# A state-space step-size tile moved from the 13th to the 9th projection tile, with its logarithm work cut in three parts

## The reference

```python
u = rmsnorm(h, norm1_w[l])
proj = u @ w_in[l]                      # 1024 -> 6672 columns
hg_q, hg_f, hg_i, hg_g, m2_z, m2_xbc, m2_dt = jnp.split(proj, PROJ_SPLITS, axis=-1)
out_a = hgrn2_mixer(hg_q, hg_f, hg_i, hg_g, ...)
out_b = mamba2_mixer(m2_z, m2_xbc, m2_dt, ...)
# inside mamba2_mixer:
xbc = jax.nn.silu(causal_dwconv(xbc, conv_w, conv_b))     # 1536 channels, 4 taps
dt = jax.nn.softplus(dt_pre + dt_bias)                    # 16 heads
da = dt * (-jnp.exp(a_log))
a_cum = jnp.cumsum(chunks of da); decay_to_end = jnp.exp(a_cum[-1] - a_cum)
```

## Time and profile before

| | |
|---|---|
| median of 3 runs | 1690.28 us (1687.13 to 1690.29) |
| the profiled execution | 1689.66 us, its span in the trace 1687.9 us |
| TensorE busy | 1314.2 us (78%), 8402 matmuls |
| VectorE busy | 514.3 us (30%) |
| ScalarE busy | 480.1 us (28%) |
| GpSimd busy | 233.5 us (14%) |
| transfers | 524.01 MB, mean 310 GB/s |

### The profile page before, as it was taken

The page is one execution under the profiler, slowest core; times in us unless marked ns, Lnnn a source line. Parts: engine busy times, 40 slices in busy tenths (PEclk is TensorE's granted clock), DMA queues, the critical chain, the costliest instruction groups (busy, mean ns, idle before and its releaser), DMA issues.

```text
span 1687.9 us, 20870 instructions
## 1 busy us (share of the span) xinstructions
PE 1314.2 (78%) x8402; PEld 777.3 (46%) x8402; DVE 514.3 (30%) x944; ACT 480.1 (28%) x725; POOL 233.5 (14%) x101
## 2 busy tenths in 40 slices
PE   8989999999999999988656667666666655666665
PEld 5877788889998988843111111111111111111111
DVE  4864667436668445622000000000000000000001
ACT  5753566436564434722100001000000100000001
POOL 0000000029777654400000000000000000000000
PEclk9999999999999999997898777888977888797888
DMA  8846332268535542286999999999999999999997
GB/s 278 330 150 242 111 101 98 70 214 274 167 138 196 213 165 100 101 337 267 428 428 428 429 429 429 428 429 428 428 429 429 428 428 429 429 429 428 429 428 299
DMA packets 93919, 524.01 MB, mean 310 GB/s; under 512 B 8057, under 2 KB 32145, under 8 KB 66081
## 3 DMA queue, kind: packets, MB, share of 16 engines
q1 hardware_dynamic: 93521, 522.61, 76.4%
q10 hardware_dynamic: 336, 0.54, 0.1%
HBM read 522.08 MB, written 1.05 MB: 310 GB/s over the span
## 4 chain that ended last, share of the span: by engine, by line
DMA 47%; PE 42%; DVE 6%; ACT 3%; issue 1%; POOL 0%; SPq 0%; DVEq 0%; ACTq 0%
DMA ring<-in_w_down 23%; DMA ring<-in_w_up 23%; PE ps L691 6%; PE ps L695 6%; PE ps L692 6%; PE ps L915 5%; PE ps L1264 3%; PE ps L939 3%; PE ps L1286 3%; PE ps L1172 2%; PE ps L675 1%; PE ps L749 1%; DVE arena L2153 1%; PE ps L845 1%; ACT ring_r L1359 1%
## 5 line engine op out<-in xcount | busy, mean ns | idle before, releaser
L1264 PE MATMUL ps<-ring,arena 128*32 128x512 f32 x1984 | 294.1, 731 | 169.7 <-DMA ring<-in_w_up 120.0
L1716 POOL TENSOR_TENSOR ring_r<-ring,ring_r 128x1024 fp32r<-128x1024 f32 (+1 forms) x96 | 232.0, 2435 | 475.2 <-ACT ring_r L1359 475.2
L691 PE MATMUL ps<-arena_r,ring_r 128*128 128x258 f32 (+3 forms) x960 | 288.9, 301 | 8.7 <-PE ps L695 3.3
L695 PE MATMUL ps<-arena_r,ring_r 128*128 128x258 f32 (+3 forms) x960 | 280.9, 293 | 0.0
L1286 PE MATMUL ps<-ring,arena 128*32 128x512 f32 x960 | 161.6, 808 | 97.6 <-DMA ring<-in_w_down 91.4
L1264 PEld LDWEIGHTS ps<-ring,arena 128*32 128x32 f32 x1984 | 62.1, 122 | 369.6 <-DMA ring<-in_w_up 184.1
L691 PEld LDWEIGHTS ps<-arena_r,ring_r 128*128 128x128 f32 x960 | 182.8, 190 | 19.5 <-issue 13.3
L695 PEld LDWEIGHTS ps<-arena_r,ring_r 128*128 128x128 f32 x960 | 182.0, 190 | 2.8
L692 PE MATMUL ps<-arena_r,ring_r 128*128 128x256 f32 (+2 forms) x608 | 180.4, 297 | 0.0
L1359 ACT ACTIVATE ring_r<-ring 128x1024 fp32r<-128x1024 f32 (+1 forms) x122 | 126.0, 1037 | 40.0 <-PE ps L692 21.4
L1718 POOL TENSOR_TENSOR arena<-arena 128x512 f32<-128x512 f32 x1 | 1.3, 1320 | 975.0 <-ACT arena L1702 975.0
(11 more groups left out here) (395 smaller groups left out, 1452.7 us busy)
## 6 DMA issues: line engine op xcount, KB each, us to landing
ring<-in_w_gate SPq DMA_DIRECT2D x64, 2048.0 KB, 26.0
ring<-in_w_down SPq DMA_DIRECT2D x63, 2048.0 KB, 26.2
ring<-in_w_up SPq DMA_DIRECT2D x60, 2048.0 KB, 24.7
ring<-in_w_in SPq DMA_DIRECT2D x20, 2048.0 KB, 11.6
ring<-in_w_ada SPq DMA_DIRECT2D x12, 2048.0 KB, 8.8
ring<-in_ffn_w_up SPq DMA_DIRECT2D x22, 1024.0 KB, 7.9
ring<-in_w_out SPq DMA_DIRECT2D x6, 2048.0 KB, 8.2
ring<-in_ffn_w_down SPq DMA_DIRECT2D x4, 2048.0 KB, 8.4
```

Source lines behind the costliest of these rows:

```text
L691: pe.matmul(o, hi[:, k, :], r_(xhi(k0 + k)), start=first and k == 0, stop=False)
L695: mm = pe.matmul(o, lo[:, k, :], r_(xhi(k0 + k)), start=False, stop=last and k == nk - 1)
L1264: mm = pe.matmul(ps[32 * j:32 * j + 32, half, :], xs[:, kt, :], wk[:, 512 * j:512 * j + 512], start=kt == 0, stop=kt == KT - 1)
L1716: pool.tensor_tensor(r_(w), w, f_(rounded(c)), ALU.subtract).then_inc(ev("w_lo"), 1)
```

## The change

The dt tile is computed ahead of p8 and not ahead of p12. ScalarE's `dt_first` comes at j = 8. VectorE's `dt_rows` becomes four functions: `dt_logs` at j = 8, `dt_steps` at j = 9, `dt_sums` at j = 11, and `dt_rows_done` (the wait for the last Exp) at j = 14. On ScalarE the last two `conv_silu`, `dt_end` and the eviction of p12 stand together at j = 13, so that Silu, Exp and Sigmoid come in blocks. The operations themselves stay the same.

```diff
-            seq += ["dt"] * (j == 12) + [f"p{j}"]
+            seq += ["dt"] * (j == 8) + [f"p{j}"]
...
-                if j == 12:
+                if j == 8:
                     pe.wait_ge(ev("small_loaded"), 16 * 8)
                     o = open_tile("dt")
...
+            def evict_projection(j):
+
+                n, m = divmod(j, 4)
+                unit_ = ORDER[n]
+                fn = {0: ACT.Silu, 1: ACT.Sigmoid, 2: ACT.Copy, 3: ACT.Silu, 4: ACT.Silu}.get(unit_ // 2, ACT.Copy)
+                evict(f"p{j}", proj[:, 4 * unit_ + m, :], T, fn)
...
-                if 2 <= j <= 13:
+                if 2 <= j <= 11:
                     conv_silu(j - 2)
+                if j == 8:
+                    dt_first()
+                if j == 13:
+                    conv_silu(10)
+                    conv_silu(11)
+                    dt_end()
+                    evict_projection(12)
                 if j == 12:
-                    dt_first()
-                if j == 14:
-                    dt_end()
+                    continue
...
-                if j == 12:
-                    dt_rows()
+                if j == 8:
+                    dt_logs()
+                if j == 9:
+                    dt_steps()
+                if j == 11:
+                    dt_sums()
+                if j == 14:
+                    dt_rows_done()
```

More of the change, by code:

```diff
@@ L1510, in gate_squares @@
                     act.activation(proj[:, TX + 4 * g + k, :], proj[:, TZ + 4 * g + k, :], ACT.Square).then_inc(ev("squares"), 1)
+            def evict_projection(j):
[3 more added lines that the diff above has]
+                evict(f"p{j}", proj[:, 4 * unit_ + m, :], T, fn)
+                act.wait_ge(ev("tiles_freed"), TN[f"p{j}"] + 1)
+                if j < 12:
+                    act.activation(m2_t[:, j % 2, :], proj[:, TX + j, :], ACT.Identity, scale=pc("m2cw", 36 + j), bias=pc("m2cb", j)).then_inc(ev("proj_tiles"), 1)
+                else:
+                    act.nop().then_inc(ev("proj_tiles"), 1)
             for j in range(NPROJ):
@@ L1529, in _ @@
                     gate_squares(0)
[L1530 to L1537, removed]
+                evict_projection(j)
             root("mz0", T)
@@ L1830, in log1p_ends, with dt_logs @@
                 st.link(tt(lg, lg, tmp, ALU.add))
-            def dt_rows():
+            def dt_logs():
                 dve.wait_ge(ev("dt_in"), 1)
@@ L1841, in dt_rows, with dt_steps @@
                 dve.nop().then_inc(ev("log_arg"), 1)
+            def dt_steps():
                 dve.wait_ge(ev("log_log"), 1)
@@ L1845, in dt_rows, with dt_sums @@
                 st.link(ts(ch(4), ch(1), chan[:, 0, 2:3], -1.0, ALU.mult, ALU.mult))
+            def dt_sums():
                 st.link(dve.tensor_tensor_scan(ch(0), cs("reset", 16)[:, 3 * T:4 * T], ch(4), 0.0, ALU.mult, ALU.add))
@@ L1857, in dt_rows, with dt_rows_done @@
                 dve.nop().then_inc(ev("m2_end"), 1)
+            def dt_rows_done():
                 dve.wait_ge(ev("row_exp"), 4)
```

## The result

The changed kernel takes 1696.53 us (median of 7 runs, 1693.89 to 1698.31), the kernel before on the same chip 1689.71 us (7 runs, 1687.13 to 1691.72). The ratio is 1.0037, 95% interval 1.0027 to 1.0046: slower by 6.8 us where 3.8 us were forecast. A second measurement, on another chip (5 runs, and 24 of the kernel before), gave 1.0042 (1.0028 to 1.0055). The profiled execution, the slowest of the seven, took 1698.31 us around a span of 1696.5 us; before the span was 1687.9 us.

The account below looks back on a forecast made before the run. Bound by TensorE from 100 to 700 us, then by the experts' weight stream from 800 us. 6.6 us lost, 3.2 and 1.1 regained (+2.35), plus 1.4 for the clock: +3.8, so 1694.1 us; range 1690.3 to 1697.3.

Parts of the forecast that it names:

- ScalarE at j = 13, p15 at 87.9 instead of 81.3: p12's eviction stands behind Silu and Exp, so p15, which needs its bank, starts late and TensorE loses 6.6 us.
- VectorE's hand-over, `conv(11)` until 83.81: VectorE, with 0.4 us per tile spare, finishes conv(11) only at 83.81; p15's subtraction alone leaves a 1.1 us gap.
- TensorE's order and ScalarE at j = 8 cost nothing: The dt work moves 14.27 us earlier at equal cost; late evictions and rounding at p8 stay hidden: 0 us.
- What comes back, 3.2 us of waits: Behind p15, TensorE's three old waits (0.4, 0.8 and 2.0 us) vanish; p15's end to the turning takes 5.8 us.
- From the turning to the states ... I take 5.43: L778 to L788 takes 5.43 us, as in the second group, instead of 6.51, regaining 1.1 us.
- The clock behind the new gap: After TensorE's gap ahead of p15 the clock dips to 1.2 GHz, costing 1.4 us (bounds 1.1 and 3.4).
- Sum: The order's balance of +2.35 us plus 1.4 us for the clock, 3.75, rounded to +3.8 us.
- Tables cost nothing: Two of ScalarE's seven table loads go (2.6 us), costed at nothing; with the skill's drain the sum would be 6.5 us.
- The spreading works: Rival, 0.12: p12 is evicted by 82.4, so p15 waits only for its subtraction; -3.1 us, 1687.2 us.
- The clock gives some back: Rival, 0.22: the gap exists, but later work misses the dip at 121.4; +2.1 us, 1692.4 us.
- Nothing reaches the end: Rival, 0.05: a later stage has 3 us of slack, so the time stays at 1690.3 us.
- The dip lasts: Rival, 0.08: the dip behind the gap is twice as long (3.4 us), or p15 waits longer; +5.8 us, 1696.1 us.

Follow-up runs that it names:

- e1: Changed kernel with p12's eviction moved ahead of the last two Silus and the last Exp on ScalarE: 1690.95 us, 1.0010 of the kernel before.
- e3: Changed kernel with VectorE's staging of turned channels put ahead of the subtraction for p20 at j = 17: 1691.07 us, 1.0007 of the kernel before.
- e4: Changed kernel with 44 matmuls that nothing reads put into TensorE's idle time ahead of p15: 1694.11 us, 1.0031 of the kernel before.
- e5: Kernel before with the grouping alone: last Silu ahead of dt_first, one pair of table loads less, dt tile unmoved: 1685.17 us, 0.9973 of the kernel before.
- e8: The changed kernel measured and traced again, unaltered, on another chip: 1696.29 us, 1.0042 of the kernel before.
- e11: Changed kernel with unread matmuls in three waits, 44 ahead of p15, 14 ahead of L788, 12 ahead of L803: 1689.91 us, 0.9996 of the kernel before.
- e7: Changed kernel with softplus and sums behind conv(11), p12 evicted before the last Exp (now j = 15), staging first at j = 17: 1686.85 us, 0.9980 of before.

## Why the prediction was right, and where its size was off

- **ScalarE at j = 13, p15 at 87.9 instead of 81.3.** Right to the tenth: 87.18 in an execution that was 0.7 us earlier, a wait of 6.4 us for the 6.6 forecast. e1 shows the cause by moving one line.
- **VectorE's hand-over, `conv(11)` until 83.81.** Right: its taps end at 83.1, with 0.15 us idle since 64.43. The small gap behind it (1.1 us) is the 1.05 us of e1.
- **TensorE's order and ScalarE at j = 8 cost nothing.** Right: no wait appears ahead of p15.
- **What comes back, 3.2 us of waits.** Right: none of the three is left.
- **"From the turning to the states ... I take 5.43".** This term failed: it measured 6.65, 1.2 us more. The prediction took the second group's row because the dip was gone, and it was gone (L778 takes 1.47 us). But it did not ask what VectorE has ahead of the staging: a subtraction that waits for ScalarE's rounding, late by the same gap. e3 removes exactly 1.23 us.
- **"The clock behind the new gap", taken at 1.4 us (1.1 to 3.4).** The mechanism held, the size was 2.5 us by p15's duration and by e4. Of the excess to L788, 2.1 us, this is what is left beside the 1.2: the path from p15's start to L778 was forecast at 9.2 us and took 11.47, 0.9 more than with the 1.4 added.
- **Sum.** 3.75 + 1.2 + 0.9 = 5.85 us up to L788; measured 5.84. The other 1.0 us of the medians, and 2.8 in the profiled execution, lie behind L788, where the changed kernel has longer and more dips than the one before and is spared the wait of 1.90 us at L1140. These were no terms of the sum; the prediction had considered only that one dip might vanish there. So that the delay at L788 reaches the end is right only in part: at 700 us it was 11.6 us and not the 5.1 of L788, and the end has 8.6 by gains and losses that nearly cancel.
- **Luck.** The time lies within the range, but not where the forecast put its weight (from 3.4 to about 5 us, at 0.53): 6.8 us is beyond that. The range reached so far up to take in a longer dip; what filled it was in part a wait at L788 that the prediction had not seen.
- **Tables cost nothing.** Right for this change: the loads that go are not on the path, the two that stay are, at 1.28 us each, and no drain on top (85.44 to 86.73). The 6.5 us that the prediction worked out with a drain lie near the measured 6.8 by chance: p15 started where the sum without it had put it. But e5 shows that the grouping can give something where the evictions stay ahead: with two loads less the turning starts 0.8 us earlier.
- **The rivals.** "The spreading works" falls at its own point: the eviction was at 86.73, not by 82.4. "The clock gives some back" fell the other way. "Nothing reaches the end" falls by the medians. "The dip lasts" came nearest in its time (1696.1), since the dip at p15 covered all of the tile, though not at twice the price alone.

Still open: why the same wait of 2.04 us has a dip behind it in the kernel before and none in e5; why VectorE's subtraction at 705 us begins behind GpSimd's in five of the traces and ahead of it in nine; and how much of the 2 to 8 us by which runs of one kernel differ is dips that come and go, since only one execution of each has a trace.

## What to carry to other kernels

When work is grouped on an in-order engine to save table loads, look first at which buffer release ends up behind the group: 2.6 us of loads were saved here and 6.4 us lost, because one PSUM bank waited for a Silu and an Exp that waited for VectorE. The grouping where no eviction became late for it measured 0.27% faster, of which its order gained 0.8 us up to the turning. Cutting a piece of work in three makes no room on an engine that has 2.62 of every 3.0 us taken. And price a new wait twice, once for its length and once for the clock behind it; where a change is worth a few tenths of a per cent, compare variants with their waits filled as well, since the dips can move with a microsecond of the order. Compare the traces at the same instruction at several places, too: a gain in the total can come from an accident far behind the change.

## What the runs showed of the hardware that was not expected

- One program had its low stretches in the same places in both of its traces (changed kernel and e8, two chips). They are about 3.4 or 6.8 us long in these kernels. A change of 1.2 us in one wait (e3) moved or removed stretches 60 us later, and some 4 us of median with them.
- Low stretches stand behind waits as short as 0.69 us (L803 at 170.63 in the changed kernel, at 163.45 in e11), 1.7 us (L803 in e7, in the changed kernel and before) and 1.96 us (changed), while a wait of 2.04 us can have none (e5).
- With 27 matmuls that nothing reads, placed ahead of two waits, the kernel before measured 1688.11 us against 1689.81 (0.9989, from 0.9979 to 1.0000), the grouped one a ratio of 0.9953 against 0.9973 on another chip (the intervals touch).
- In all 14 traces one 128x512 subtraction of VectorE at about 705 us took 0.69 us where it began 0.14 to 0.15 us ahead of a GpSimd subtraction (nine) and 2.79 to 2.81 us where it began 0.13 to 0.14 us behind it (five), with a wait of 1.9 us on TensorE in those five alone.
